# All six levels' masks ahead of the inverse, with homes of their own, and wider rings for the S5 states

## The reference

```python
for l in range(DEPTH):                       # DEPTH = 2
    x = x + 0.5 * swiglu(rms_norm(x), ...)   # d_ff 2816
    x = x + hybrid_mixer(rms_norm(x), ...)
    x = x + 0.5 * swiglu(rms_norm(x), ...)
return rms_norm(x)
```

```python
lower = where(strict, beta * (k @ k.T) * decay, 0)
sol = triangular_solve(lower, rhs, unit_diagonal=True)
```

```python
x_t = abar * x_(t-1) + bbar u_t              # complex, 16 groups of 64 states
y = c_re @ x_re - c_im @ x_im + d * u
```

## Time and profile before

| | |
|---|---|
| median of 3 runs | 1333.11 us (1332.14 to 1333.88) |
| the profiled execution | 1334.75 us, of which 1333.0 us are its span |
| PE busy | 1301.6 us, 98% |
| DVE busy | 930.6 us, 70% |
| ACT busy | 659.6 us, 49% |
| POOL busy | 230.0 us, 17% |
| mean granted clock of TensorE | 0.996 |

### The profile page before, as it was taken

How to read it: one execution, slowest core, us unless ns; L and a number is a source line. 1 busy time by engine, 2 the same in 40 slices (tenths; PEclk the granted TensorE clock), 3 DMA queues, 4 the chain that set the end, 5 groups by cost and what they waited for, 6 DMA issues and landing times. The chain is left out here.

```text
span 1333.0 us, 27445 instructions
## 1 busy us (share of the span) xinstructions
PE 1301.6 (98%) x11728; PEld 1266.9 (95%) x11728; DVE 930.6 (70%) x1435; ACT 659.6 (49%) x953; POOL 230.0 (17%) x183
## 2 busy tenths in 40 slices
PE   8999999999999999999999999999999999999997
PEld 8899999998888999999999999999978899999997
DVE  5788675896857866666658885567788588566654
ACT  6544646753234464444455446477422455544542
POOL 1000011004834610000100000100166263000000
PEclk9999999999999999999999999999999999999999
DMA  5655564544132556556545555545422345455562
GB/s 196 239 170 198 188 195 140 173 155 132 65 127 95 168 174 197 187 188 228 190 159 190 190 184 195 176 152 166 159 96 73 120 141 185 160 186 187 181 216 91
DMA packets 61465, 220.24 MB, mean 165 GB/s; under 512 B 6944, under 2 KB 7200, under 8 KB 60960
## 3 DMA queue, kind: packets, MB, share of 16 engines
q1 hardware_dynamic: 61344, 218.50, 49.6%
HBM read 217.42 MB, written 1.05 MB: 164 GB/s over the span
## 5 line engine op out<-in xcount | busy, mean ns | idle before, releaser
L447 PE MATMUL bank<-xh,whi 128*128 128x256 f32 x2256 | 638.4, 283 | 8.6 <-DVE wlo L1303 7.5
L448 PE MATMUL bank<-xl,whi 128*128 128x256 f32 x2256 | 631.2, 280 | 0.0
L449 PE MATMUL bank<-xh,wlo 128*128 128x256 f32 x2256 | 630.9, 280 | 0.0
L1303 DVE TENSOR_TENSOR wlo<-raw,whi 128x1024 fp32r<-128x1024 f32 (+1 forms) x384 | 469.2, 1245 | 229.3 <-ACT whi L905 227.9
L905 ACT ACTIVATE whi<-raw 128x1024 fp32r<-128x1024 f32 (+1 forms) x414 | 419.8, 1035 | 176.6 <-PE bank L449 98.1
L447 PEld LDWEIGHTS bank<-xh,whi 128*128 128x128 f32 x2256 | 425.1, 188 | 15.5 <-issue 8.4
L448 PEld LDWEIGHTS bank<-xl,whi 128*128 128x128 f32 x2256 | 425.2, 188 | 0.2
L449 PEld LDWEIGHTS bank<-xh,wlo 128*128 128x128 f32 x2256 | 425.0, 188 | 0.0
L449 PE MATMUL bank<-hh,wlo 128*128 128x256 f32 x704 | 197.0, 280 | 0.0
L447 PE MATMUL bank<-hh,whi 128*128 128x256 f32 x704 | 196.7, 279 | 0.0
L448 PE MATMUL bank<-hl,whi 128*128 128x256 f32 x704 | 196.6, 279 | 0.0
(11 more groups left out here) (366 smaller groups left out, 1445.8 us busy)
## 6 DMA issues: line engine op xcount, KB each, us to landing
raw<-weights SPq DMA_DIRECT2D x350, 512.0 KB, 3.8
raw<-weights SPq DMA_DIRECT2D x64, 448.0 KB, 4.0
cst<-consts SPq DMA_DIRECT2D x1, 1088.0 KB, 8.2
par<-params SPq DMA_DIRECT2D x1, 1072.5 KB, 8.7
par<-params SPq DMA_DIRECT2D x1, 1060.5 KB, 9.5
x<-x_in SPq DMA_DIRECT2D x2, 512.0 KB, 7.7
y_out<-ret SPq DMA_DIRECT2D x4, 256.0 KB, 2.3
ropec<-positions SPq DMA_DIRECT2D x1, 128.0 KB, 8.7
```

The lines of the kernel that those rows point to most:

```text
L447: mm(out, w[0], a[0], start=start, stop=False)
L448: mm(out, w[0], a[1], start=False, stop=False)
L449: return mm(out, w[1], a[0], start=False, stop=stop)
L1303: V.tensor_tensor(slot(wlo, i), slot(raw, i), r32(slot(whi, i)), ALU.subtract).then_inc(S("low_dve"), 1)
```

## The change

Each level gets a home of its own for its masked blocks, in parts of `big` that are free at the time. All twelve mask instructions of a layer are issued ahead of the inverse. Their waits are now for DVE's last write of `low` (`bb0`, `bb1`, L1677), only the last level's for `qk0`, `qk1`, since its home is the former `dec`. The scans get three buffers instead of two, the turned-back states four instead of two. The outputs of the groups 2lv-2 and 2lv-1, which PE had at the end of level lv, now stand in level lv+1 behind the xy product of the first half set.

```diff
-        lowc = dec
+        lowc = [big[:, c:c + 4 * P].rearrange("p (h t j c) -> p h t j c", h=2, t=2, j=2) for c in (512, 1536, 4096, 4608, 5632, 0)]
+        scanned = (tmpC, tmpD, flat8[:, 0:2, :])
+        turned = (tmpE, tmpF, tmpB, flat8[:, 2:4, :])
...
@@ s5_out(s), on PE
-                xs = (tmpE, tmpF)[s % 2]
+                xs = turned[s % 4]
...
@@ the levels, on PE
                         last.then_inc(S("side"), 1)
+                    if hp == 0 and lv >= 2:
+                        s5_out(2 * lv - 4)
+                        s5_out(2 * lv - 3)
                 if lv < 4:
                     s5_in(2 * lv)
                     s5_in(2 * lv + 1)
-                if 0 < lv < 5:
-                    s5_out(2 * lv - 2)
-                    s5_out(2 * lv - 1)
...
@@ level_blocks(lv), on POOL
                 for hp in range(2):
-                    if lv == 0:
-                        pool.wait_ge(S("side_dve"), side.taken(f"qk{hp}"))
-                    elif lv == 1:
-                        pool.wait_ge(S("y_first"), hp + 1)
-                    else:
-                        pool.wait_ge(S("side"), side.ready(f"t{hp}_{lv - 1}"))
+                    pool.wait_ge(S("side_dve"), side.taken(f"qk{hp}" if lv + 1 == LEVELS else f"bb{hp}"))
...
@@ s5_back(s), on POOL
-                ss, xs = (tmpC, tmpD)[s % 2], (tmpE, tmpF)[s % 2]
+                ss, xs = scanned[s % 3], turned[s % 4]
...
-                if s >= 2:
-                    pool.wait_ge(*since("s5y", s - 1))
+                if s >= 4:
+                    pool.wait_ge(*since("s5y", s - 3))
...
-            for lv in range(LEVELS):
-                if lv + 1 < LEVELS:
-                    level_blocks(lv + 1)
-                if lv + 2 == LEVELS:
-                    pool.wait_ge(*since("lowc", 2 * LEVELS))
-                    nc.gpsimd.memset(state, 0.0).then_inc(S("state_zero"), 1)
-                if lv < 4:
-                    s5_back(2 * lv)
-                    s5_back(2 * lv + 1)
+            for lv in range(1, LEVELS):
+                level_blocks(lv)
+            nc.gpsimd.memset(state, 0.0).then_inc(S("state_zero"), 1)
+            for st in range(NST):
+                s5_back(st)
...
@@ s5_state(s), on DVE
-                ss = (tmpC, tmpD)[s % 2]
-                if s >= 2:
-                    dve.wait_ge(*since("s5x", s - 1))
+                ss = scanned[s % 3]
+                if s >= 3:
+                    dve.wait_ge(*since("s5x", s - 2))
```

More of the change, by code:

```diff
@@ L731, in tensor_layer @@
                         for r in chunks:
-                            a, b = (my[r, hp, t, j, :], ident[r, r]) if lv == 0 else (lowc[r, hp, t, j, :], mx[r, hp, t, j, :])
+                            a, b = (my[r, hp, t, j, :], ident[r, r]) if lv == 0 else (lowc[lv][r, hp, t, j, :], mx[r, hp, t, j, :])
                             last = mm(ps[r, i * 64:(i + 1) * 64], a, b, start=True, stop=True)
@@ L1222, in level_blocks @@
                 for hp in range(2):
-                    if lv == 0:
-                        pool.wait_ge(S("side_dve"), side.taken(f"qk{hp}"))
-                    elif lv == 1:
-                        pool.wait_ge(S("y_first"), hp + 1)
-                    else:
-                        pool.wait_ge(S("side"), side.ready(f"t{hp}_{lv - 1}"))
-                    tt(lowc[:, hp].rearrange("p t j c -> p (t j) c"), low[:, hp].rearrange("p t j c -> p (t j) c"),
+                    pool.wait_ge(S("side_dve"), side.taken(f"qk{hp}" if lv + 1 == LEVELS else f"bb{hp}"))
+                    tt(lowc[lv][:, hp].rearrange("p t j c -> p (t j) c"), low[:, hp].rearrange("p t j c -> p (t j) c"),
                        over(lev[:, lv, 0:64], 4), ALU.mult).then_inc(S("lowc"), 1)
             def s5_back(s):
-                ss, xs = (tmpC, tmpD)[s % 2], (tmpE, tmpF)[s % 2]
+                ss, xs = scanned[s % 3], turned[s % 4]
                 pool.wait_ge(*since("s5s", s + 1))
@@ L1267, in pool_layer @@
                 pool.wait_ge(*since("lowc", hp + 1))
-                tt(my[:, hp].rearrange("p t j c -> p (t j) c"), over(chunk_ident, 4), lowc[:, hp].rearrange("p t j c -> p (t j) c"),
+                tt(my[:, hp].rearrange("p t j c -> p (t j) c"), over(chunk_ident, 4), lowc[0][:, hp].rearrange("p t j c -> p (t j) c"),
                    ALU.subtract).then_inc(S("y_first"), 1)
-            for lv in range(LEVELS):
-                if lv + 1 < LEVELS:
-                    level_blocks(lv + 1)
-                if lv + 2 == LEVELS:
-                    pool.wait_ge(*since("lowc", 2 * LEVELS))
-                    nc.gpsimd.memset(state, 0.0).then_inc(S("state_zero"), 1)
-                if lv < 4:
-                    s5_back(2 * lv)
-                    s5_back(2 * lv + 1)
+            for lv in range(1, LEVELS):
[3 more added lines that the diff above has]
+                s5_back(st)
             low_parts(["g11", "g12", "g13"])
```

## The result

| | before | after |
|---|---|---|
| median | 1332.62 us (4 runs, 1331.51 to 1333.88) | 1319.34 us (4 runs, 1317.76 to 1319.73) |
| profiled execution, its span | 1334.75, 1333.0 us | 1319.73, 1317.2 us |
| mean granted clock | 0.996 | 0.996 |

After over before is 0.9895, with a 95% interval of 0.9883 to 0.9906: 12.5 to 15.6 us less. The two medians alone are 13.3 us apart. The forecast was 1318.6, in a range of 1315.8 to 1324.6.

What follows compares the result with a forecast made beforehand. PE's queue was taken as the bound, busy 1301.6 of 1333.0 us. With DVE pacing the levels, gains of 8.0 and 6.5 sum to 14.5 us: 1334.75 becomes 1320.2, the median 1318.6, range 1315.8 to 1324.6.

Steps and rivals of the forecast that it cites:

- The seam: End of level 1: PE passes straight into level 2, outputs half a level later without waiting, both taking 0.99 us.
- rival B: At the outputs: only the listed waits and the lower clock go, 9.6 us, giving 1323.5; chance 0.2 with its surroundings.
- DVE as the pace: Level stage: DVE's queue sets 11.97 us a level; gains 8.0 and 6.5, sum 14.5 us; chance 0.62.
- the best case of 16.6: Level stage: PE alone sets the pace at 11.32 us a level, gaining 9.0 and 7.6 us in the two layers.
- DVE's hold: PE waits on DVE through the bank of xy0, so level 5 begins 1.0 us later than with PE alone.
- The second rotary product: Level 4: it waits until DVE has read xy0, then takes 0.96 us, with PE waits of up to 1 us.
- The masks: POOL ahead of the inverse: 12 masks in one run, done by 315, cost 0; removing them alone shortens no wait.
- The buffers: Scan and turned-back state buffers: more are needed because outputs come later, but by themselves cost and win nothing.
- POOL's slack: At the outputs: POOL's pair of groups takes 10.09 us under DVE's 11.97, leaving 1.2 us in every level.
- The SBUF rule: DVE beside POOL: the loser is blocked for the whole instruction; a pair takes 11.4 us, losing 0.1 us a level.
- The clock: PE's granted clock stays at its upper level through the levels.
- after level 5: From level 5 to the layer's end: what follows waits on PE's position in turn; no give-back counted.

Runs made afterwards that it cites:

- xy0 first: Changed kernel, but in levels 1 to 4 DVE subtracts xy0 before making the `wlo` of the next gate's first half; 1319.27 us, ratio 0.9890.
- masks-only: Kernel before with all masks ahead into own homes, but outputs at the end of their own level and rings as before; 1331.64 us, ratio 1.0000.
- last outputs late: xy0 first, plus outputs of groups 6 and 7 behind the second xy of level 5; 1316.2 us, ratio 0.9858, again 1316.19, 0.9880.
- rings of two: Changed kernel with two buffers each, as before, for the scans and the turned-back states; 1320.48 us, ratio 0.9907.
- POOL longer: Changed kernel with one more POOL product in each `s5_back`, written to columns nobody reads; 1327.49 us, ratio 0.9963.
- outputs only: Changed kernel with the masks back in one home between the groups, outputs and rings staying as changed; 1336.7 us, ratio 1.0024.
- eleven dummies: Changed kernel with eleven unread 128x128 identity products on PE in its wait ahead of the state product; 1322.51 us, ratio 0.9906.

## Why the prediction was right

**The seam.** The mechanism came as forecast. PE was to pass the seam straight into level 2, and both outputs were to take 0.99 half a level later. They take 1.00 and wait for nothing. "The outputs would have to lose their overlap" (rival B) did not happen.

**DVE as the pace.** The forecast was 11.97 a level, measured 11.84. The `wlo` stayed at 1.69 us, as POOL stayed beside them; the 0.13 less lies in the two groups of `s5_state`, 7.42 us for the 7.55 of the earlier trace rows. Level 5 was put at 364.87 and 1019.04; it began at 361.35 and 1007.90. The start-up made the whole stage 3.7 us earlier in layer 0, and 364.87 - 3.68 = 361.19, 0.16 off. In distance from the first `s5_in`, level 5 gained 8.98 by the forecast and 8.82 measured in layer 0, 7.53 and 7.37 in layer 1 (the gains of 8.0 and 6.5 are these less the pair of outputs that level 5 now holds; at the `u` product they are 7.74 and 6.30). So 14.0 came for the 14.5: 0.16 us a layer are missing in the levels, and 0.09 in the pair of outputs, which costs 1.08 at the `u` product and not 0.99.

**Details of the step that were off.** PE's own level was put at 11.32 us, read from the old order; in the new one it is 11.45, as the kernel with xy0 first shows, so the best case of 16.6 was about 0.4 us a layer too large. Of DVE's hold, 1.0 us up to level 5 by the forecast, 0.8 came: 0.4 in each of levels 2 and 3. The second `s5_in` product was taken to cost 0.53 us behind the bank's release; from the end of the read (336.09) to T (337.20) it is 1.11, hand-over included, for my 0.63. The shorter DVE level made up for part of it. The second rotary product was to wait as well; it does not (1.92 us from 359.43 to 361.35, as when free).

**The masks.** Forecast: one run, done by 315, free of cost. They were done by 307.6. The `wlo` beside them took 2.79 and 3.05 us for two, where two took 2.39 and 2.85 before, so DVE lost 0.6 us in its idle stretch. "Taking them away shortens no wait by itself" is what the masks-only kernel shows. What the prediction did not say is that the gain of moving the outputs would be lost without them.

**The buffers.** "That is needed" does not hold: without the wider rings the kernel works and about 1 us a layer is lost. "It costs and wins nothing by itself" was not tested; no run has the rings alone.

**POOL's slack** was put at 1.2 us in every level. It is 1.6 in the first three pairs and 0.8 in the last, whose L1241 takes 1.08 us for 0.64 and whose L1242 takes 1.19 for 0.74. The 4.46 us that I called the free time of a group were not free: its last product stood beside a `wlo` and took 1.12 us, where it takes 0.73 without one, so a free group is 3.9 us. Two free groups and two `wlo` of 1.22 make 10.3 us, and 10.2 are measured: POOL loses about the whole time of both `wlo`. The SBUF rule that I weighed against the rows (the Trainium skill, "SBUF — State Buffer", "Who interferes with whom": the loser of the shared port is blocked for the whole instruction) gave a pair of 11.4 us only because of that 4.46; worked out with the free group, its estimate is the same 10.3, and the trace agrees in the sum. It does not show that one of the two goes on undisturbed: side by side L1297 takes 1.69 us for 1.22 and POOL's L1238 2.07 for 1.27.

**The clock** was to stay at its upper level through the levels. It did, but past the stage it fell once, in layer 1, 1.5 us that the prediction had as zero under "after level 5". The start-up's 3.7 us in the other direction are the profiled pair's: in the fourteen kept profiles the first `s5_in` of layer 0 stands anywhere between 311.9 and 317.0 us. That the median came within 0.7 us of the forecast, 1319.34 for 1318.6, is in part luck: the same kernel's median was 1316.3 and 1319.7 in its later runs. What the forecast can be held to is the stage, 14.0 for 14.5.

## What to carry to other kernels

Where an in-order engine waits for a piece whose consumer is not urgent, move the piece back by the producer's lateness, and look in the same pass for what else stands behind that producer: here the masks sat in the same queue, and the move alone made the kernel slower. Compute the new pace from the next engine's unbroken level, then the slack of the third, and ask what the third's instructions do to the next one's when they fall side by side; each of the three limits here (POOL's seam, DVE's bank, POOL's last group) hid the next one: freeing the bank would have given 1.4 us a layer, and POOL took 1.1 of it back. And measure a change in one stage by distances inside it, since one and the same kernel's spans lay 6 us apart.

## What the runs showed of the hardware

The clock does not always answer a pause in the same way. Behind the pause of about 1.3 us ahead of the state product it fell in 9 of 16 layers in eight profiles without dummies (three of the changed kernel, two of the last outputs late, one each of xy0 first, rings of two and POOL longer), in none of 6 layers of the kernel before, outputs only and masks only, and in none of 6 with dummies in it. Each fall cost some 1.5 us. The order of the engine's instructions around the pause is the same in all of these but for the dummies; what decides between them, I don't know. How often it happens in executions that were not profiled is not shown either: their mean granted clock is 0.996 to 0.999 with eleven dummies and 0.995 to 0.999 in the changed kernel beside it, which does not tell them apart. Behind the pause of 2.0 us at the end of level 1 it fell in 3 of 4 layers (the kernel before and masks only). Behind the 3.61 us pause of the outputs-only kernel it fell in both layers, and there it cost 2.2 us in layer 0 (a level of 13.64 for 11.45).

VectorE (DVE) and GpSimd (POOL) slow each other down by an amount that depends on which of their instructions meet. A `wlo` (128x1024, both inputs in SBUF) takes 1.22 us without POOL, 1.69 beside it in the changed kernel, and up to 2.25 in the kernels with rings of two and with POOL longer; a scan of DVE (L1692) takes 0.67 us and up to 1.27.
